# Attention probabilities turned by DVE in squares of 32 rows, row sums divided on ACT, values taken three pieces behind the scores

## What is computed

```python
def forgetting_attention(q, k, v, log_f):
    c = jnp.cumsum(log_f, axis=1).transpose(0, 2, 1)
    for i in range(s // Q_BLOCK):                      # two blocks of 128 queries
        q0 = i * Q_BLOCK
        kl = q0 + Q_BLOCK
        logits = einsum('bqhd,bkhd->bhqk', q[:, q0:kl], k[:, :kl]) * scale
        logits = logits + c[:, :, q0:kl, None] - c[:, :, None, :kl]
        logits = where(causal, logits, -inf)
        probs = softmax(logits, axis=-1)
        outs.append(einsum('bhqk,bkhd->bqhd', probs, v[:, :kl]))
...
p = h @ w_in_odd[o]                                    # q, k, v of 2048 columns each, 16 forget columns
att = forgetting_attention(q, k, v, log_f)
mix = att @ w_out_odd[o]
```

## Time and profile before

| | before |
|---|---|
| median of 3 runs | 2101.39 us (2101.27 to 2101.73) |
| profiled execution | 2101.76 us, span 2100.0 us |
| PE busy | 2087.7 us, 99% |
| DVE busy | 1493.8 us, 71% |
| ACT busy | 1045.8 us, 50% |
| POOL busy | 30.2 us, 1% |
| HBM read | 394.29 MB, 189 GB/s over the span |

### The profile page before, as it was taken

How to read it: one execution, slowest core, us unless ns; L and a number is a source line. 1 busy time by engine, 2 the same in 40 slices (tenths; PEclk the granted TensorE clock), 3 DMA queues, 4 the chain that set the end, 5 groups by cost and what they waited for, 6 DMA issues and landing times.

```text
span 2100.0 us, 29629 instructions
## 1 busy us (share of the span) xinstructions
PE 2087.7 (99%) x11034; PEld 1802.7 (86%) x11034; DVE 1493.8 (71%) x1692; ACT 1045.8 (50%) x1078; POOL 30.2 (1%) x59
## 2 busy tenths in 40 slices
PE   9999999999999999999999999999999999999998
PEld 7888888888888888888888888888888888888886
DVE  6788786777667776776556655977776767767677
ACT  7554564445444454455444444554454444444454
POOL 0000000000000000000101000000000000000000
PEclk9999999999999999999999999999999999999999
DMA  8655565555555555564665555565655556555552
GB/s 300 198 172 196 168 216 192 190 196 186 187 198 182 200 180 190 196 196 154 197 187 175 186 176 187 171 207 184 200 180 188 193 181 209 188 180 198 181 194 106
DMA packets 317298, 397.16 MB, mean 189 GB/s; under 512 B 8724, under 2 KB 240956, under 8 KB 317116
## 3 DMA queue, kind: packets, MB, share of 16 engines
q1 hardware_dynamic: 313500, 391.27, 56.3%
q0 software_dynamic: 1056, 3.16, 0.7%
q10 hardware_dynamic: 2688, 1.99, 0.3%
HBM read 394.29 MB, written 2.11 MB: 189 GB/s over the span
## 4 chain that ended last, share of the span: by engine, by line
PE 99%; DMA 0%; DVE 0%; SPq 0%; ACT 0%; issue 0%; DVEq 0%; ACTq 0%
PE ps_turned L1335 39%; PE ps_straight L1374 36%; PE ps_turned L1344 20%; DMA x<-in_x 0%; PE ps_turned L1406 0%; PE ps_straight L1627 0%; PE ps_straight L1644 0%; PE ps_straight L1636 0%; PE ps_straight L1507 0%; PE ps_straight L1654 0%; PE ps_turned L1583 0%; PE ps_turned L1579 0%; PE ps_straight L1583 0%; PE ps_straight L1579 0%; PE ps_turned L1578 0%; PE ps_straight L1578 0%
## 5 line engine op out<-in xcount | busy, mean ns | idle before, releaser
L842 DVE TENSOR_TENSOR w_low<-w_raw,w_high 128x2048 fp32r<-128x2048 f32 x369 | 846.1, 2294 | 402.1 <-ACT w_high L459 364.2
L459 ACT ACTIVATE w_high<-w_raw 128x2048 fp32r<-128x2048 f32 x368 | 704.9, 1918 | 667.9 <-PE ps_straight L1374 293.2
L1335 PE MATMUL ps_turned<-h_split,w_high 128*128 128x512 f32 x3584 | 832.2, 390 | 0.0
L1335 PEld LDWEIGHTS ps_turned<-h_split,w_high 128*128 128x128 f32 x3584 | 667.6, 188 | 135.3
L1344 PEld LDWEIGHTS ps_turned<-h_split,w_low 128*128 128x128 f32 x3584 | 440.7, 192 | 6.1 <-issue 0.2
L1344 PE MATMUL ps_turned<-h_split,w_low 128*128 128x256 f32 x3584 | 445.3, 283 | 0.0
L1374 PE MATMUL ps_straight<-w_high,y_split 128*128 128x512 f32 x1856 | 440.5, 390 | 0.0
L1374 PEld LDWEIGHTS ps_straight<-w_high,y_split 128*128 128x128 f32 x1856 | 347.9, 188 | 72.0
L1374 PE MATMUL ps_straight<-w_low,y_split 128*128 128x512 f32 x928 | 229.2, 389 | 0.0
L1374 PEld LDWEIGHTS ps_straight<-w_low,y_split 128*128 128x128 f32 x928 | 174.2, 188 | 36.2
L1075 DVE SCALAR_TENSOR_TENSOR work<-work,conv_columns 128x256 f32<-128x256 f32 x352 | 154.6, 480 | 10.9
(11 more groups left out here) (204 smaller groups left out, 609.6 us busy)
## 6 DMA issues: line engine op xcount, KB each, us to landing
w_raw<-in_w_up SPq DMA_DIRECT2D x176, 1024.0 KB, 5.0
w_raw<-in_w_down SPq DMA_DIRECT2D x88, 1024.0 KB, 5.0
w_raw<-in_w_in_odd SPq DMA_DIRECT2D x48, 1024.0 KB, 5.3
w_raw<-in_w_in_even SPq DMA_DIRECT2D x23, 1024.0 KB, 5.4
w_raw<-in_w_out_even SPq DMA_DIRECT2D x16, 1024.0 KB, 5.0
w_raw<-in_w_out_odd SPq DMA_DIRECT2D x16, 1024.0 KB, 5.0
work<-c_rows POOLq DMA_DIRECT2D x8, 256.0 KB, 4.5
x<-in_x SPq DMA_DIRECT2D x3, 512.0 KB, 11.2
```

What stands on the lines that cost most here:

```text
L459: a.activation(wh[:, s, :], raw[:, s, :], ACT.Copy).then_inc(s_high, 1)
L842: ve.tensor_tensor(wl[:, s, :], raw[:, s, :], wh[:, s, :].bitcast(F32), ALU.subtract).then_inc(s_low, 1)
L1335: ins = pe.matmul(psT[:, 2 * slot + m, :], hi[:, kk, P * m:P * m + P], acts[:, K, :], start=(K == 0 and not narrow_ran), stop=(K == KC - 1 ...
```

## The change

The three PE transposes of each head and the ACT copy out of PSUM go away (`turn_probs`, `head_probsT`). In their place DVE turns `probs` into `probsT` in squares of 32 x 32 (`head_blocks`): 16 `transpose` instructions for a head, each over 32 partitions and three runs of 32 columns (32 x 96), which move block row i, block column j to block row j, block column i. It waits for `s_pr` and for `attend` of the head before, which frees `probsT`. The two multiplications by the inverted row sums move from DVE to ACT (`head_scale`, right behind `head_exp`); DVE keeps the reciprocal (`head_inverse`), which now stands behind the `low` of its step instead of ahead of it. In DVE's program `head_low` moves by one step. `attend` moves one step later on PE, to three pieces behind the scores, except for heads 13 and 15 in the tail: head 13 moves from n = 0 to n = 1 and is again three behind, head 15 stays at n = 4, two pieces after its scores. ACT's copy of v (`s_vr`) moves from k = 5 to k = 7. The bank for turned probabilities is not used any more.

```diff
@@ -715,11 +715,11 @@
                 fenced(a.activation(probs[:, P:3 * P], probs[:, P:3 * P], ACT.Exp, bias=nmax[:, 1:2],
                                     accum_out=rsum[:, 1:2]), s_exp, at(hh + 1, 4, r))
-            def head_probsT(hh, bank, r=0):
-                a.wait_ge(s_pt, at(hh + 1, 4, r))
-                if not (isinstance(r, int) and hh == 0):
-                    a.wait_ge(s_att, at(hh, 4, r))
-                fenced(a.activation(probsT, bank[:, 0:3 * P], ACT.Copy), s_ptc, at(hh + 1, 4, r))
+            def head_scale(hh, r=0):
+                a.wait_ge(s_inv, at(hh + 1, 4, r))
+                a.activation(probs[:, 0:P], probs[:, 0:P], ACT.Copy, scale=rinv[:, 0:1])
+                fenced(a.activation(probs[:, P:3 * P], probs[:, P:3 * P], ACT.Copy, scale=rinv[:, 1:2]), s_pr,
+                       at(hh + 1, 4, r))
             def head_high(hh, bank, r=0):
                 a.wait_ge(s_att, at(hh + 1, 4, r))
@@ -743,16 +743,10 @@
                         a.wait_ge(s_fl, 1)
                         link(a.activation(fe, fe, ACT.Exp))
                         fenced(a.activation(fe, fe, ACT.Ln, bias=1.0), s_fe, 1)
-                    if first and k in (0, 2, 4):
-                        head_probsT(hh - 3 + k // 2, psA[:, 3, :], r)
-                    if first and k in (1, 3, 5):
-                        head_high(hh - 3 + k // 2, psA[:, 3, :], r)
-                    if k == 10:
-                        head_probsT(hh, psA[:, 3, :], r)
-                    if k == 11:
-                        head_high(hh, psA[:, 3, :], r)
+                    if first and k in (0, 2, 4, 6):
+                        head_high(hh - 4 + k // 2, psA[:, 3, :], r)
                     high(c + k + LEAD, r)
-                    if k == 5:
+                    if k == 7:
                         a.wait_ge(s_used, at(c + 4, 12, r))
                         if first == 0:
                             a.wait_ge(s_rstd, 3)
@@ -763,8 +757,10 @@
                         fenced(ins, s_vr, at(first + 1, 1, r))
                     if first and k in (1, 3):
                         head_exp(hh - 2 + k // 2, r)
+                        head_scale(hh - 2 + k // 2, r)
                     if k in (9, 11):
                         head_exp(hh + (k - 9) // 2, r)
+                        head_scale(hh + (k - 9) // 2, r)
                     if k in (5, 7, 9, 11):
                         j = (k - 5) // 2
                         copy_low_half(Q_MIX1 + 4 * first + j, j % 2, c + k, r)
@@ -772,21 +768,16 @@
             heads_of_group(0)
             with a.Fori(0, 3) as r:
                 heads_of_group(1, r)
-            OB, PB, O14 = psT[:, 3, :], psT[:, 3, :], psT[:, 1, :]
             for k in range(16):
-                if k == 0:
-                    head_probsT(13, psA[:, 3, :])
-                if k == 1:
-                    head_high(13, O14)
-                if k in (2, 4):
-                    head_probsT(13 + k // 2, PB)
-                if k in (3, 5):
-                    head_high(13 + k // 2, OB)
+                if k in (0, 2, 4, 5):
+                    h = {0: 12, 2: 13, 4: 14, 5: 15}[k]
+                    head_high(h, {12: psA[:, 3, :], 13: psT[:, 1, :]}.get(h, psT[:, 3, :]))
                 if k in (9, 11, 14):
                     turned_high(3, {9: 0, 11: 1, 14: 2}[k])
                 high(N_OUT1 + k + LEAD)
                 if k in (1, 3):
                     head_exp(14 + k // 2)
+                    head_scale(14 + k // 2)
                 if k in (7, 8, 12):
                     squares(3, {7: 0, 8: 1, 12: 2}[k])
             ffn(1)
@@ -1180,8 +1171,6 @@
                 ve.wait_ge(s_sc, at(hh + 1, 4, r))
                 ve.wait_ge(s_bias, at(hh // 2 + 1, 2, r))
-                if not (isinstance(r, int) and hh == 0):
-                    ve.wait_ge(s_pt, at(hh, 4, r))
                 for t in range(2):
                     a0, a1 = (0, P) if t == 0 else (P, 3 * P)
                     ins = ve.scalar_tensor_tensor(out=probs[:, a0:a1], in0=bank[:, a0:a1],
@@ -1192,12 +1181,22 @@
                 link(ve.tensor_reduce(rmax[:, 1:2], probs[:, P:3 * P], AX_X, ALU.max))
                 fenced(ve.tensor_scalar(nmax, rmax, -1.0, None, ALU.mult), s_mx, at(hh + 1, 4, r))
-            def head_probs(hh, r=0):
+            def head_inverse(hh, r=0):
                 ve.wait_ge(s_exp, at(hh + 1, 4, r))
-                link(ve.reciprocal(rinv, rsum))
-                ve.tensor_scalar(probs[:, 0:P], probs[:, 0:P], rinv[:, 0:1], None, ALU.mult)
-                fenced(ve.tensor_scalar(probs[:, P:3 * P], probs[:, P:3 * P], rinv[:, 1:2], None, ALU.mult),
-                       s_pr, at(hh + 1, 4, r))
+                fenced(ve.reciprocal(rinv, rsum), s_inv, at(hh + 1, 4, r))
+
+            def head_blocks(hh, r=0):
+
+
+                ve.wait_ge(s_pr, at(hh + 1, 4, r))
+                if not (isinstance(r, int) and hh == 0):
+                    ve.wait_ge(s_att, at(hh, 4, r))
+                for i in range(4):
+                    for j in range(4):
+                        src = probs[32 * i:32 * i + 32, :].rearrange("p (n j b) -> p n j b", n=3, j=4)[:, :, j, :]
+                        dst = probsT[32 * j:32 * j + 32, :].rearrange("p (n i b) -> p n i b", n=3, i=4)[:, :, i, :]
+                        ins = ve.transpose(dst, src)
+                fenced(ins, s_ptc, at(hh + 1, 4, r))
             def head_low(hh, bank, r=0):
                 ve.wait_ge(s_atthi, at(hh + 1, 4, r))
@@ -1214,17 +1213,18 @@
                         turned_low(2, 3)
                         mean_square(2)
                         spread_rstd(2)
-                    if first and k in (1, 3, 5):
-                        head_low(hh - 3 + k // 2, psA[:, 3, :], r)
-                    if first and k in (1, 3):
-                        head_logits(hh - 2 + k // 2, psA[:, 2, :], r)
-                        head_probs(hh - 2 + k // 2, r)
-                    if k == 11:
-                        head_low(hh, psA[:, 3, :], r)
-                    if k in (9, 11):
-                        head_logits(hh + (k - 9) // 2, psA[:, 2, :], r)
-                        head_probs(hh + (k - 9) // 2, r)
+                    if first and k in (0, 2, 4, 6):
+                        head_low(hh - 4 + k // 2, psA[:, 3, :], r)
+                    if first and k in (0, 2, 4):
+                        head_blocks(hh - 3 + k // 2, r)
+                    if k == 10:
+                        head_blocks(hh, r)
+                    h = hh - 2 + k // 2 if first and k in (1, 3) else hh + (k - 9) // 2 if k in (9, 11) else None
+                    if h is not None:
+                        head_logits(h, psA[:, 2, :], r)
                     low(c + k + LEAD, r)
+                    if h is not None:
+                        head_inverse(h, r)
                     if first == 0 and k == 1:
                         take_rstd(2)
                         link(ve.tensor_scalar(q_rstdT, rstdT[:, :], float(P) ** -0.5, None, ALU.mult))
@@ -1255,16 +1255,18 @@
                 assert chain["n"] == before + HEAD_LINKS, chain["n"] - before
                 chain.update(n=before + HEAD_LINKS * 3, r=0, step=0)
             for k in range(16):
-                if k == 1:
-                    head_low(13, psT[:, 1, :])
-                if k in (3, 5):
-                    head_low(13 + k // 2, psT[:, 3, :])
+                if k in (0, 2, 4, 5):
+                    h = {0: 12, 2: 13, 4: 14, 5: 15}[k]
+                    head_low(h, {12: psA[:, 3, :], 13: psT[:, 1, :]}.get(h, psT[:, 3, :]))
+                if k in (0, 2, 4):
+                    head_blocks(13 + k // 2)
                 if k in (1, 3):
                     head_logits(14 + k // 2, psT[:, 2, :])
-                    head_probs(14 + k // 2)
                 if k in (9, 11, 14):
                     turned_low(3, {9: 0, 11: 1, 14: 2}[k])
                 low(N_OUT1 + k + LEAD)
+                if k in (1, 3):
+                    head_inverse(14 + k // 2)
                 if k in (6, 7, 11, 15):
                     c = {6: 0, 7: 1, 11: 2, 15: 3}[k]
                     add_to_x(A_OUT1 + c, c, N_OUT1 + k)
@@ -1627,18 +1629,11 @@
                 pe.matmul(bank[:, P:3 * P], qT[:, m, P:TOK], kT[:, m, :], start=False, stop=True,
                           skip_group_check=True).then_inc(s_sc, 1)
-            def turn_probs(hh, bank, r=0):
-
-                pe.wait_ge(s_pr, at(hh + 1, 4, r))
+            def attend(hh, bank, group, r=0):
+
+                pe.wait_ge(s_ptc, at(hh + 1, 4, r))
                 if not (isinstance(r, int) and hh == 0):
                     pe.wait_ge(s_attlo, at(hh, 4, r))
-                for b in range(3):
-                    ins = pe.transpose(bank[:, P * b:P * b + P], probs[:, P * b:P * b + P], ident[:, :])
-                ins.then_inc(s_pt, 1)
-
-            def attend(hh, bank, group, r=0):
-
-                pe.wait_ge(s_ptc, at(hh + 1, 4, r))
```

(26 more changed lines are left out.)

## The result

The changed kernel takes 2105.37 us (median of 22 runs, 2103.73 to 2106.04), the kernel before 2101.33 us (22 runs): ratio 1.0018, 95% interval 1.0012 to 1.0023. That is 4.0 us more, at the edge of the 0.2% that was set as no change. 2102.3 us was forecast, in a range of 2096.4 to 2109.5.

The account below looks back on a forecast made before the run. PE, busy 99% of the span, was taken as the bound. From the profiled 2101.8 us, -5.2 (transposes) +4.3 (tail wait) +1.8 (loop waits, signal) gave 2102.7, or 2102.3 us for the median; range 2096.4 to 2109.5.

Parts of the forecast that it names:

- PE loses 5.2 us: On PE's chain, the three transposes of each of 16 heads go, 0.325 us a head, 5.2 us in all.
- A head's squares take 4.53 us: On DVE, 16 transposes of 32x96 for each head at 0.283 us each, 4.53 us.
- the first rival: All hidden: a square takes 0.21 us or less on DVE, no wait is left, 2096.2 us; chance 0.2.
- The tail waits 4.3 us at head 15: In the tail, PE is ready for attend of head 15 after 42.5 us, its squares after 46.8: 4.3 us.
- The loop waits 0.8 us twice: In the loop's second and third pass, PE waits about 0.8 us before attend of heads 7 and 11.
- ACT's share costs 0.78 us: ACT gains two scalings for each head, taken as 0.78 us for both.
- The clock: Rival: behind PE's standstill of over 4 us the clock drops for one piece, adding 5.5 us, 2107.8 us; chance 0.07.
- A wait costs its length: In the sum, PE's waits were added at their length: 4.3 us in the tail, 1.8 in the loop with the signal.

Follow-up runs that it names:

- e4: The kernel before, with the three PE transposes of each head done twice, 48 more: 2106.53 us, ratio 1.0025.
- e3: The changed kernel with 8 of the 16 squares of a head left out: 2095.84 us, ratio 0.9973 to the kernel before.
- e5: The changed kernel; in DVE's tail the low halves of pieces 3 to 6 each one step later: 2102.23 us, ratio 1.0002 to the kernel before.
- e6: The changed kernel; in DVE's tail two low halves kept behind the squares of head 15: 2098.49 us, ratio 0.9986 to the kernel before.
- e8: The changed kernel with DVE again multiplying by the inverted row sums, ACT doing no scaling: 2098.15 us, ratio 0.9986 to the kernel before.
- e7: e6 plus, in each loop pass, the low halves of pieces 3 to 6 one step later: 2096.68 us, ratio 0.9977 to the kernel before.
- e9: The changed kernel with the edits of e8 and e5 together: 2096.41 us, ratio 0.9975 to the kernel before.
- e2: The changed kernel with 20 products into an unused bank ahead of attend of head 15 in the tail: 2103.23 us, ratio 1.0007 to the kernel before.

## Why the prediction was right or wrong

- *PE loses 5.2 us.* Right, and a little small: 4.9 us by e4's median and 5.8 by e3's, 5.3 and 5.4 by their traces.
- *A head's squares take 4.53 us.* Right: 4.51 to 4.53 us, 270 ns each and 0.28 apart, with no overlap, as in the earlier trace rows. The per-column rate of another operation served to shorten it. This was what decided against the first rival.
- *The tail waits 4.3 us at head 15.* Right: 4.4 us, at that head and for the reason named. The count behind it holds too: from the end of piece 9 (1256.15) the squares of head 15 were done after 46.7 us (46.8 forecast) and PE was ready after 42.4 us (42.5). e5, e6 and e8 shortened the series by known amounts, and the wait followed.
- *The loop waits 0.8 us twice.* Nearly: 0.6 us twice, and about even at head 3.
- *ACT's share costs 0.78 us.* Right in size, but no step asked what the division would cost where it was; e8 shows that this part of the change alone brings its waits in the loop and 2.6 us of that in the tail.
- *The clock.* This step failed: the forecast let the granted clock stay as it was. The mechanism was named and given 0.07, because the trace of before shows no such gap and keeps its clock over the 1.9 us at the start. It happens behind the wait in the profile, and no run of the changed kernel came as low as the kernel that filled the gap. Its price was put at one piece at half speed, 5.5 us; it was 2.3, as the slow clock lasted 6.8 us and PE stood still for 1.9 us of them. The forecast contained the wait of over 4 us itself, so the forecast and this rival were not alternatives: the rival was the consequence of it.
- *A wait costs its length.* So the forecast's sum took it; the restart was missing, 0.27 us each time, four times.

Together: 2101.3 - 5.4 + 5.7 + 1.1 + 2.3 = 2105.0 us, against 2105.4 measured. For the profiled executions the account closes at their distance of 3.7 us. The 0.4 us left between the medians are there because the profiled execution of the kernel before lay 0.4 us above its median, as the prediction says, and that of the changed kernel within 0.1 us of its own. In e6, e7 and e9 0.4 us of what they are over their expected times lie at head 15; the remaining 0.2 to 0.5 us were not found. The start of the kernel differs by as much between executions: the first low half begins at 13.39 us in e9 and at 14.19 in e2.

The forecast of 2102.3 lacks the clock and the restarts, 3.4 us, and is 0.6 us too high in waits and transposes together. That the measured time still lies in the stated range is in part luck: the range was made wide for the price of a square, and that price came out as forecast.

## What to carry to other kernels

Where PE never waits, count what it is relieved of by the spacing on the chain, and then lay out the other engines' steps in series up to the instant at which PE needs them: the slack is the difference of two sums of some 45 us, and DVE's 74% busy says nothing of it. Fewer changes of engine in such a series can be worth more than less work; a step that is not needed soon (here the low half of a later piece) should stand behind the series. A wait of PE has to be priced with the restart, and a longer one with the clock: behind 4.4 us the clock fell in the profiled execution, and behind 2.2 and 1.8 us 7 and 3 of 11 executions were slower, which is inferred to be the same. Where the wait of 4.4 us stayed, filling it with idle products was 2.1 us cheaper than leaving it open.

## What was not expected of the hardware

The granted clock went to 0.50 within a wait of 4.4 us and stayed there some 4 us after PE had taken up work. With a wait of 2.2 us seven runs in 11 were 1.7 us longer, with 1.8 us three in 11, with 1.0 us and less no such group showed, and at the kernel's start 1.9 us passed at full clock. So a short wait makes the time of a kernel uncertain and not only longer.
